# Two layers on one core: 64 tokens by fetched rows and 192 dense, with two weight parts in one stationary operand

## The reference, cut to what matters

```python
def _peer(h, w_query, sub_keys, expert_u, expert_v):
    q = (h @ w_query).reshape(B, S, PEER_HEADS, 2, PEER_KEY_DIM)      # 8 heads
    sc = jnp.einsum('bshpk,hpnk->bshpn', q, sub_keys)
    ...
    idx = jnp.take_along_axis(cand_idx, pos, axis=-1)                # 16 experts per head
    g = jax.nn.softmax(top_s, axis=-1)
    ...
        act = jax.nn.gelu(jnp.einsum('td,tkd->tk', xt, expert_u[it]))
        return jnp.einsum('tk,tkd->td', gt * act, expert_v[it])
```

## Time and profile before

| | |
|---|---|
| median of 3 runs | 1867.45 us (1861.47 to 1868.68) |
| the profiled execution | 1863.85 us |
| its span in the trace | 1862.5 us |
| mean granted TensorE clock | 0.93 |
| busy share of PE, DVE, ACT, POOL | 84%, 52%, 34%, 33% |
| DMA | 482.38 MB, 259 GB/s mean |

### The profile page before, as it was taken

The page is one execution under the profiler, slowest core; times in us unless marked ns, Lnnn a source line. Parts: engine busy times, 40 slices in busy tenths (PEclk is TensorE's granted clock), DMA queues, the critical chain, the costliest instruction groups (busy, mean ns, idle before and its releaser), DMA issues.

```text
span 1862.5 us, 21544 instructions
## 1 busy us (share of the span) xinstructions
PE 1559.8 (84%) x8662; PEld 1159.0 (62%) x8662; DVE 973.5 (52%) x1488; ACT 642.4 (34%) x924; POOL 609.5 (33%) x379
## 2 busy tenths in 40 slices
PE   6889989889888888799899999999797666666665
PEld 5677844334233323687789999999696544444443
DVE  5653512011010001566453787886227999887787
ACT  5453411001000001456453444443247634323333
POOL 3111100000000000322131434434645788888880
PEclk8988999999999999899999999999899888777777
DMA  7322578998998999444343566666862399989895
GB/s 255 115 89 68 204 288 368 422 421 357 421 421 356 422 421 407 136 142 152 113 139 133 183 209 197 205 207 198 303 194 93 136 353 345 346 314 338 304 361 222
DMA packets 110184, 482.38 MB, mean 259 GB/s; under 512 B 13808, under 2 KB 22512, under 8 KB 68480
## 3 DMA queue, kind: packets, MB, share of 16 engines
q1 hardware_dynamic: 85696, 408.04, 58.6%
q0 software_dynamic: 22528, 67.19, 10.0%
q10 hardware_dynamic: 1856, 5.72, 0.8%
HBM read 468.84 MB, written 12.06 MB: 258 GB/s over the span
## 4 chain that ended last, share of the span: by engine, by line
PE 58%; POOL 12%; DMA 10%; DVE 7%; issue 6%; ACT 6%; ACTq 0%; SPq 0%; DVEq 0%
PE ps L619 14%; PE ps L452 11%; PE ps L453 10%; PE ps L454 10%; POOL small L2307 6%; POOL big L2292 6%; DMA fix<-in_w_up 4%; PE ps L668 3%; DMA big<-in_w_up 3%; PE ps L640 2%; DMA big<-in_expert_v,tig 1%; DVE fix_parts L1040 1%; DMA fix<-in_expert_v 1%; PE ps L582 1%; PE ps L1017 1%
## 5 line engine op out<-in xcount | busy, mean ns | idle before, releaser
L454 PE MATMUL ps<-hh_parts,fix_parts 128*128 128x256 f32 x1152 | 328.6, 285 | 0.0
L619 PE MATMUL ps<-big 128*64 128x512 f32 x880 | 249.6, 602 | 30.0 <-DMA big<-in_w_up 13.2
L1040 DVE TENSOR_TENSOR fix_parts<-fix,fix_parts 128x1536 fp32r<-128x1536 f32 (+1 forms) x101 | 209.0, 2070 | 121.0 <-ACT fix_parts L1845 118.8
L1017 PE MATMUL ps<-fix_parts,y_parts 128*128 128x512 f32 x428 | 180.6, 493 | 81.6 <-DVE big_parts L1696 81.5
L1845 ACT ACTIVATE fix_parts<-fix 128x2048 fp32r<-128x2048 f32 x101 | 193.1, 1913 | 155.9 <-DMA fix<-in_expert_v 145.8
L452 PE MATMUL ps<-hh_parts,fix_parts 128*128 128x256 f32 x768 | 221.2, 288 | 20.2 <-issue 16.5
L2267 POOL TENSOR_TENSOR fix_parts<-fix,fix_parts 128x512 fp32r<-128x512 f32 x58 | 140.0, 2415 | 264.6 <-ACT fix_parts L1845 264.6
L454 PEld LDWEIGHTS ps<-hh_parts,fix_parts 128*128 128x128 f32 x1152 | 223.7, 194 | 0.0
L453 PE MATMUL ps<-hl_parts,fix_parts 128*128 128x256 f32 x768 | 219.6, 286 | 0.0
L619 PE MATMUL ps<-fix,big 128*64 128x512 f32 x656 | 197.1, 595 | 22.2 <-DMA fix<-in_w_up 7.3
L2267 POOL TENSOR_TENSOR big_parts<-big,fix_parts 128x512 fp32r<-128x512 f32 x12 | 23.7, 1974 | 546.4 <-ACT fix_parts L1845 546.4
(11 more groups left out here) (369 smaller groups left out, 3098.5 us busy)
## 6 DMA issues: line engine op xcount, KB each, us to landing
fix<-in_expert_u SPq DMA_DIRECT2D x64, 1024.0 KB, 5.1
fix<-in_expert_v SPq DMA_DIRECT2D x64, 1024.0 KB, 7.4
big<-in_w_down SPq DMA_DIRECT2D x38, 1024.0 KB, 11.1
big<-in_w_gate SPq DMA_DIRECT2D x36, 1024.0 KB, 11.1
big<-in_w_up SPq DMA_DIRECT2D x36, 1024.0 KB, 9.6
fix<-in_w_gate SPq DMA_DIRECT2D x28, 1024.0 KB, 11.2
fix<-in_w_up SPq DMA_DIRECT2D x28, 1024.0 KB, 9.6
fix<-in_w_down SPq DMA_DIRECT2D x26, 1024.0 KB, 11.1
```

The costliest lines, as they stand in the source:

```text
L454: return pe.matmul(o, l[1], r[0], start=False, stop=last)
L619: ins = pe.matmul(m.PS[64 * i:64 * i + 64, bank, :], lhs(h * k_of // 2 + k, i), view(t.place[t.slot[x]])[:, k, c0:c0 + 512], start=(h + k ...
L1017: ins = pe.matmul(m.PS[:, half, :], w[x][:, j, :], v[y][:, at:at + 512], start=(i + j + x + y == 0), stop=(i == 63 and j + x == 2), skip_g ...
L1040: nc.vector.tensor_tensor(m.fr(x[:, 0:end]), x[:, 0:end], m.fr(hi[:, 0:end]).bitcast(F32), ALU.subtract).then_inc(s.lo_v, 1)
```

## The change

The split of tokens moves from 128 and 128 to 64 and 192, and the product of the dense part is laid out anew.

- Sparse part: 64 tokens. "sparse" makes three 64x128 lists (rows, activation places, gates) in L3. ACT waits for them at tile 23 and moves them by two DMAs to a 128x64 form, so that partition t and partition 64 + t each serve half of token t's 128 experts. There are 64 fetches and 64 picks instead of 128 each. All picks are issued ahead of the fetches beyond the ring, and the ring has 5 buffers instead of 14. `sum_at` starts with step 3 and gives about one row sum to a step.
- Dense part: 192 tokens. "share" and "keys" run for block 0 too, the one-hot stage has 48 steps instead of 32, W has 192 columns an expert pair row instead of 128, and less goes to `actkeep`.
- The product over `expert_v`: ACT and DVE write the high and low parts of W (now 128x384) interleaved into WP, high, low, high, low. For the first 64 dense tokens the 128 interleaved columns are one stationary operand, and two passes (over the high and the low part of the tile) give all products. They go to two PSUM banks of their own, with a token's two parts on neighbouring partitions. The other 128 dense tokens take three passes as before, with every second column of WP as stationary operand. That is 8 + 12 = 20 matmuls a tile.
- The end: DVE copies the row sums and ACT the interleaved sums out of PSUM, and PE joins partition pairs by four matmuls with 64 columns of weights (F). Block 1's residual is added first, block 0's behind the join.

```diff
-RING = 14
+SPARSE = 64
+DENSE = 192
+RING = 5
...
-    ROUTING[_at + 22] = [("keys", _b, 0) if _b else ("sparse", 0, 0)]
+    ROUTING[_at + 22] = [("keys", _b, 0)] + [("sparse", 0, 0)] * (1 - _b)
...
-    return 1 + a * 62 // P
+    return 3 + a * 60 // SPARSE
...
-    m.W = BIG[:, 0:16384].rearrange("p (n t) -> p n t", n=128)
-    m.keys = tuple(m.tig[:, P * i:P * i + P] for i in range(3))
-    m.vix, m.aix, m.sg = m.tig[:, 384:512].bitcast(U32), m.tig[:, 512:640].bitcast(U32), m.tig[:, 640:768]
-    m.ROWS = [BIG[:, o:o + 1024] for o in [*range(24576, 32768, 1024), *range(16384, 22528, 1024)]]
-    m.ST = [BIG[:, o:o + 256].rearrange("p (n t) -> p n t", n=2) for o in (22528, 22784)]
+    m.W = BIG[:, 0:128 * DENSE].rearrange("p (n t) -> p n t", n=128)
+    m.keys = tuple(m.tig[:, DENSE * i:DENSE * i + DENSE] for i in range(3))
+    lists = m.tig[:, 3 * DENSE:768]
+    m.lists = lists.rearrange("p (x k) -> p x k", x=3)
+    m.vix, m.aix, m.sg = lists[:, 0:64].bitcast(U32), lists[:, 64:128].bitcast(U32), lists[:, 128:192]
+    m.ROWS = [DS[:, 3072 + 1024 * i:4096 + 1024 * i] for i in range(RING)]
...
+    m.ST = [yf[:, 1792 + 128 * i:1920 + 128 * i].rearrange("p (n t) -> p n t", n=2) for i in range(2)]
...
-    m.WH = [yf[:, 512 * i:512 * i + 256] for i in range(3)]
+    m.WP = [DS[:, 768 * i:768 * i + 768] for i in range(3)]
+    m.F = [EB[1][:, 1024 + 64 * i:1088 + 64 * i] for i in range(2)]
+    m.PARTS = m.ROWS[0:2]
...
-    return m.W[:, 2 * i:2 * i + 2, :].rearrange("p n t -> p (n t)")
+    two = m.fr(m.WP[i % 3]).rearrange("p (c x) -> p x c", x=2)
+    return m.W[:, 2 * i:2 * i + 2, :].rearrange("p n t -> p (n t)"), two[:, 0, :], two[:, 1, :]
...
         for what, b, _ in ROUTING.get(i, ()):
-            if what == "share" and b:
-                pe.wait_ge(s.r_share, 2)
+            if what == "share":
+                pe.wait_ge(s.r_share, b + 1)
+                if b:
+                    pe.wait_ge(s.r_keys, 1)
                 for n, src in enumerate((m.r_i1, m.r_i2, m.r_gg)):
                     ins = pe.transpose(m.PS[:, 6, n * P:(n + 1) * P], src, m.ident)
                 ins.then_inc(s.r_turned, 1)
...
-    for q in range(32):
+    for q in range(DENSE // 4):
...
-        w = [m.fr(x).rearrange("p (n t) -> p n t", n=2) for x in (m.WH[i % 3], w_tile(m, i))]
+        both = m.fr(m.WP[i % 3]).rearrange("p (j c) -> p j c", j=2)
+        w = m.fr(m.WP[i % 3]).rearrange("p (j c x) -> p j x c", x=2, j=2)
         for j in range(2):
             for half in range(2):
-                at = 1024 * j + 512 * half
+                for y in range(2):
+                    ins = pe.matmul(m.PS[:, 2 + half, :], both[:, j, 0:128], v[y][:, 1024 * j + 512 * half:1024 * j + 512 * half + 512],
+                                    start=(i + j + y == 0), stop=(i == 63 and j + y == 2), skip_group_check=True)
+        if i == 63:
+            ins.then_inc(s.half, 1)
+        for j in range(2):
+            for half in range(2):
                 for x, y in ((0, 0), (0, 1), (1, 0)):
-                    ins = pe.matmul(m.PS[:, half, :], w[x][:, j, :], v[y][:, at:at + 512],
+                    ins = pe.matmul(m.PS[:, half, :], w[:, j, x, 64:DENSE], v[y][:, 1024 * j + 512 * half:1024 * j + 512 * half + 512],
                                     start=(i + j + x + y == 0), stop=(i == 63 and j + x == 2), skip_group_check=True)
         ins.then_inc(s.used, 2)
+
+    pe.wait_ge(s.fold, 1)
+    pe.wait_ge(s.parts, 2)
+    for half in range(2):
+        for j in range(2):
+            ins = pe.matmul(m.PS[64 * j:64 * j + 64, 4 + half, :], m.F[j], m.PARTS[j][:, 512 * half:512 * half + 512],
+                            start=True, stop=True, skip_group_check=True)
+    ins.then_inc(s.joint, 1)
...
-    ve.wait_ge(s.r_keys, 1)
+    ve.wait_ge(s.r_keys, 2)
...
-    weigh(31)
+    weigh(DENSE // 4 - 1)
+    ve.wait_ge(s.ghot, DENSE // 4)
+    v.step(ve.tensor_tensor(m.F[0], m.ident[:, 0:64], m.ident[:, 64:128], ALU.add))
+    pairs = m.ident.rearrange("p (c x) -> p x c", x=2)
+    ve.tensor_tensor(m.F[1], pairs[:, 0, :], pairs[:, 1, :], ALU.add).then_inc(s.fold, 1)
 
     def w_low(i):
-        w = w_tile(m, i)
+        w, hi, lo = w_tile(m, i)
         ve.wait_ge(s.w_hi, i + 1)
-        ve.tensor_tensor(m.fr(w), w, m.fr(m.WH[i % 3]).bitcast(F32), ALU.subtract).then_inc(s.w_lo, 1)
+        ve.tensor_tensor(lo, w, hi.bitcast(F32), ALU.subtract).then_inc(s.w_lo, 1)
...
-    ve.wait_ge(s.summed, P)
+    ve.wait_ge(s.summed, SPARSE)
+    ve.tensor_copy(m.PARTS[0], SUM).then_inc(s.parts, 1)
+    ve.wait_ge(s.used, t.used[-1])
     ve.wait_ge(s.fin_in, 32)
-    for b in range(2):
-        if b:
-            ve.wait_ge(s.used, t.used[-1])
+    for b in (1, 0):
+        if b == 0:
+            ve.wait_ge(s.joint, 1)
         for half in range(2):
             xb = m.XB[:, b, 512 * half:512 * half + 512]
-            ve.tensor_tensor(xb, xb, m.PS[:, 6 - 6 * b + half, :], ALU.add).then_inc(s.y_sq, 1)
+            ve.tensor_tensor(xb, xb, m.PS[:, 4 - 4 * b + half, :], ALU.add).then_inc(s.y_sq, 1)
...
+        if b and n == 0:
+            ve.wait_ge(s.moved, 32)
...
-        ve.wait_ge(s.r_turned, 1)
+        ve.wait_ge(s.r_turned, b + 1)
+        n, to = ((SPARSE, 0), (0, P - SPARSE))[b]
         for i, dst in enumerate(m.keys):
-            ins = ve.tensor_copy(dst, m.PS[:, 6, i * P:(i + 1) * P])
+            ins = ve.tensor_copy(dst[:, to:to + P - n], m.PS[:, 6, i * P + n:(i + 1) * P])
         ins.then_inc(s.r_keys, 1)
...
     elif what == "sparse":
-        lines, quad, sums, place, diag = m.LI
-        lines = lines.bitcast(U32)
-        v.step(ve.tensor_copy(lines, m.r_i2))
-        v.step(ve.tensor_tensor(diag, m.ident, m.iota, ALU.mult))
+        h = lambda x: x[0:SPARSE]
+        i1, i2 = h(m.r_i1), h(m.r_i2)
+        lines, row, at = (h(m.L3[:, x, :]) for x in range(3))
+        u, quad, sums, place = (h(x) for x in m.LI)
...
-        v.step(ve.tensor_copy(m.sg, m.r_gg))
-        ve.tensor_copy(m.vix, sums).then_inc(s.lists, 1)
+        v.step(ve.tensor_copy(lines.bitcast(U32), sums))
+        ve.tensor_copy(at, h(m.r_gg)).then_inc(s.lists, 1)
...
+            elif what == "sparse":
+                ac.wait_ge(s.lists, 1)
+                for x in range(2):
+                    ac.dma_start(m.lists[64 * x:64 * x + 64], m.L3[0:64, :, 64 * x:64 * x + 64]).then_inc(s.moved, 16)
...
-        ac.activation(m.ST[i % 2], src[:, :, 0:P], ACT.Gelu_apprx_tanh)
-        ac.activation(m.W[:, 2 * i:2 * i + 2, :], src[:, :, P:256], ACT.Gelu_apprx_tanh).then_inc(s.act, 1)
+        ac.activation(m.ST[i % 2], src[:, :, 0:SPARSE], ACT.Gelu_apprx_tanh)
+        ac.activation(m.W[:, 2 * i:2 * i + 2, :], src[:, :, SPARSE:256], ACT.Gelu_apprx_tanh).then_inc(s.act, 1)
...
-    ac.wait_ge(s.ghot, 32)
+    ac.wait_ge(s.ghot, DENSE // 4)
...
-        ac.activation(m.fr(m.WH[i % 3]), w_tile(m, i), ACT.Copy).then_inc(s.w_hi, 1)
-
-    ac.wait_ge(s.weighed, 32)
-    ac.wait_ge(s.e_a, 32)
+        w, hi, _ = w_tile(m, i)
+        ac.activation(hi, w, ACT.Copy).then_inc(s.w_hi, 1)
...
-    ac.wait_ge(s.used, t.used[-1])
-    for b in range(2):
-        ac.wait_ge(s.y_sq, 2 * b + 2)
+    ac.wait_ge(s.half, 1)
+    ac.wait_ge(s.summed, SPARSE)
+    ac.activation(m.PARTS[1], m.PS[:, 2:4, :].rearrange("p a n -> p (a n)"), ACT.Copy).then_inc(s.parts, 1)
+    for b in (1, 0):
+        ac.wait_ge(s.y_sq, 4 - 2 * b)
...
-    po.wait_ge(s.lists, 1)
-    po.wait_ge(s.r_keys, 1)
+    po.wait_ge(s.r_keys, 2)
+    po.wait_ge(s.moved, 32)
     for k in range(RING):
         fetch(k)
     for n in range(first + 53, first + 64):
...
-    def pick(k):
-
+    for k in range(SPARSE):
         po.indirect_dma_start(m.pk[:, k:k + 1], None, acts,
                               bass.IndirectOffsetOnAxis(m.aix[:, k:k + 1], 0)).then_inc(s.picked[k // 16], 16)
-
-    for k in range(32):
-        pick(k)
-    for k in range(P):
-        if k + 32 < P:
-            pick(k + 32)
-        if k + RING < P:
-            po.wait_ge(s.summed, k + 1)
-            fetch(k + RING)
+    for k in range(RING, SPARSE):
+        po.wait_ge(s.summed, k - RING + 1)
+        fetch(k)
...
-            sy.dma_start(actkeep[:, 256 * n:256 * n + 256], m.ST[n % 2].rearrange("p n t -> p (n t)")).then_inc(s.acts_kept[n % 2], 16)
+            sy.dma_start(actkeep[:, 128 * n:128 * n + 128], m.ST[n % 2].rearrange("p n t -> p (n t)")).then_inc(s.acts_kept[n % 2], 16)
```

42 lines of the change are left out of this document (24 added, 18 removed).

## The result

| | before | changed |
|---|---|---|
| median, same chip | 1863.18 us (8 runs, 1858.82 to 1868.68) | 1872.94 us (7 runs, 1868.34 to 1883.11) |
| ratio | | 1.006, 95% interval 1.0034 to 1.0087 |
| profiled execution, its span | 1863.85, 1862.5 us | 1879.67, 1878.3 us |

An eighth run of the changed kernel fell into a slower state of the chip (1948.9 us, granted clock 0.946 for 0.964 to 0.972) and is left out of the median and the ratio. The change makes the kernel slower by 0.6%. The forecast was 1850 us, with 1832 to 1868 as its own range, so its direction is wrong and the time lies outside that range (inside the wider one of 8 in 10, 1808 to 1895). I cut the stages in all kernels at the same places: the first and the last gelu of `expert_u` on ACT, the first and the last matmul of the `expert_v` stage on PE.

The account below looks back on a forecast made before the run. It took POOL's pairs of indirect DMAs to bound the expert_v stage, with a slot ring nearly as long behind. Terms -38 + 27.4 - 14.5 + 4.8 + 0.4 + 2.3 = -17.6 gave 1850 us, range 1832 to 1868.

Parts of the forecast that it names:

- One-hots: One-hot stage: 16 more steps at 1.71 us, all on the path, +27.4 us.
- Sparse part: Last stage: POOL's 211 us saved leave the path; fetch 5 still fits, 0 to 3 us, taken as 0.
- Ring fetches: expert_u stage: five fetches hold POOL 6.6 us, PE loses 1.9 us instead of 16.4, -14.5 us.
- Lists: expert_u stage, tile 23: ACT's wait for DVE's lists delays gelus and high part, +4.8 us, from 0 to 7.
- The interleaved operand: expert_v stage: loading every second column for 12 of 20 matmuls hides under the matmuls, 0 us.
- The rival on it: expert_v stage: interleaving adds 0.8 us on PE and 0.55 on DVE a step, 1880 us in all; chance 0.09.
- PE's 20 matmuls: expert_v stage: 20 matmuls for 12 a tile, at full clock 0.23 us each, 4.6 us.
- PE at the clock of now: expert_v stage: 0.33 us a matmul, 6.6 us a tile, PE the limit, 1927 us in all; chance 0.05.
- The ring: expert_v stage: a tile's stations sum to 16.3 us, 5.4 a step over three slots, -38 us (-73 to +11).
- The ring doesn't shorten: expert_v stage: landing stays 7.4 us and DVE's queue 1.8, step 6.2, 1899 us in all; chance 0.16.
- PE full: expert_v stage: landing 5.1 us, no DVE queue, step 4.6 to 4.9 us, say 1815 us in all; chance 0.18.
- Tail: End of the kernel: four joining matmuls stand behind PE's last tile, +2.3 us, from 1 to 4.

Follow-up runs that it names:

- e14: The changed kernel with one plain float32 matmul of 512 columns on PE behind each tile's release but the last; 1868.94 us, ratio 1.0042.
- e9: The changed kernel, three slots, with 24 instead of 20 matmuls a tile; 1877.66 us against 1864.9.
- e2: The changed kernel without the 59 fetches behind the first five, row sums reusing the first rows; 1825.89 us against 1864.43.
- e1: The changed kernel with a fourth slot for expert_v tiles; 1808.11 us against 1864.43, ratio 0.9698.
- e7: The kernel before with 16 picks and 14 fetches in place of 128 each; 1809.72 us against 1860.76.
- e6: The kernel before with a fourth slot for expert_v tiles; 1857.98 us, ratio 0.9978.
- e8: The changed kernel with ACT's wait for the lists moved from tile 23 to tile 30; 1866.39 us against 1860.76.
- e11: The changed kernel with two plain float32 matmuls of 512 columns behind each tile's release but the last; 1909.98 us against 1869.17.

## Why a three-slot ring stood at 5.8 us

I took each tile's stations from the starts in the timelines of PE, ACT and DVE, for 61 tiles:

| mean, us | predicted | changed | e14 | e9 (24) | e2 (no fetch) |
|---|---|---|---|---|---|
| slot released to ACT's start (landing) | 6.4 | 6.48 | 6.29 | 5.74 | 5.15 |
| ACT high part | 1.9 | 1.91 | 1.91 | 1.91 | 1.91 |
| queue ahead of DVE | 0.5 | 0.25 | 0.17 | 0.12 | 0.07 |
| DVE low part | 2.3 | 2.29 | 2.29 | 2.29 | 2.29 |
| W's low part, hand-over | 0.6 | 0.62 | 0.62 | 0.62 | 0.62 |
| queue ahead of PE | 0 | 0.92 | 0.89 | 0.97 | 0.15 |
| PE | 4.6 | 4.95 | 4.95 | 5.60 | 4.69 |
| a third of the sum | 5.4 | 5.81 | 5.71 | 5.75 | 4.96 |

(e14's PE row has the end of the filler in it; the prediction's 6.4 is its 6.2 of landing and 0.2 of hand-overs.) The mean landing was foretold well. What the sum left out is the queue at PE, 0.92 us, in a stage where PE also idles 0.93 us a step. (That the measured stations add up to three steps proves nothing by itself: they do so in any ring, with the waiting counted in. What tells is where the waiting stands, and what a fourth slot does to it.) Both at once can only be when tiles arrive unevenly. They do, and this stretch shows how. PE first (one tile ends, a gap, the next):

```profile
1609.34 0.40 PE L1035 MATMUL ps<-x_parts,big_parts 128*128 128x512 f32 x1
1613.32 3.75 PE L1028 MATMUL ps<-fix_parts,big_parts 128*128 128x512 f32 x8 [3.59 <-DVE big_parts L1726]
1616.87 4.08 PE L1035 MATMUL ps<-fix_parts,big_parts 128*128 128x512 f32 x12
1620.79 1.53 PE L1028 MATMUL ps<-fix_parts,big_parts 128*128 128x512 f32 x6
```

ACT, which takes up a tile as it lands:

```profile
1600.00 1.92 ACT L1882 ACTIVATE x_parts<-fix 128x2048 fp32r<-128x2048 f32 x1 [6.72 <-DMA fix<-in_expert_v]
...
1608.47 1.92 ACT L1882 ACTIVATE fix_parts<-fix 128x2048 fp32r<-128x2048 f32 x1 [6.10 <-DMA fix<-in_expert_v]
...
1611.10 1.91 ACT L1882 ACTIVATE fix_parts<-fix 128x2048 fp32r<-128x2048 f32 x1 [0.28 <-DMA fix<-in_expert_v]
...
1616.70 1.91 ACT L1882 ACTIVATE x_parts<-fix 128x2048 fp32r<-128x2048 f32 x1 [3.25 <-DMA fix<-in_expert_v]
```

and DVE's row sums and POOL's fetches:

```profile
1596.17 2.68 DVE L1742 SCALAR_TENSOR_TENSOR ps<-big,small,ps 128x1024 f32<-128x1024 f32 x2
```

```profile
1597.73 0.94 POOL L2336 DMA_INDIRECT big<-in_expert_v,tig  x1 [1.33 <-DVE ps L1742]
1599.12 0.94 POOL L2336 DMA_INDIRECT big<-in_expert_v,tig  x1 [0.45 <-DVE ps L1742]
```

DVE does two row sums in a row, so POOL issues two fetches, 1.4 us apart, and the slot is released while the second is being issued, at 1599.54 (where PE is through with the tile three back). The tile lands after 8.9 us, at 1608.5, the next one 2.6 us behind it. PE has idled for 3.6 us and takes the late tile at 7.47 us for 4.6; the tile behind it has been ready for 3.6 us when PE gets to it at 1620.79. A late tile lengthens the turn of its slot, and the tile that then waits lengthens the turn of the next; an early one gives nothing back, since its slot can't be filled before PE is through.

How often? For each tile I counted the fetches whose issue on POOL ended between 2 us before its slot was released and 2.5 us before ACT's start:

| fetches beside the landing | changed | e9 (24) | e14 | e1 (four slots) |
|---|---|---|---|---|
| none | 24 tiles, 5.52 us | 18, 5.41 | 22, 5.34 | 8, 5.78 |
| one | 22, 6.64 | 34, 5.63 | 26, 6.35 | 21, 7.39 |
| two or three | 15, 7.78 | 9, 6.83 | 13, 7.77 | 31, 8.32 |
| over 6.5 us | 32 of 61 | 12 of 61 | 24 of 61 | 51 of 60 |

In the changed kernel each fetch of 0.5 MB beside a tile of 1 MB goes with about 1.1 us more of landing, and two fifths of the tiles have none beside them. These are counts within a run; the run that takes the fetches away is e2. There the landing is 5.15 us, 6.75 at most, and of queue and gaps 0.15 and 0.34 us a step are left. With four slots the landings are longer than ever, 7.7 us on average, and PE's gaps are down to 0.05 us a step: a slot more is what a ring needs to carry uneven landings.

Why 24 matmuls cost no more than 20 with three slots follows in part. In e9 PE runs without a gap from the fortieth tile on, at 5.53 us a step and landings of 5.1 to 5.7 us, though the fetches go on: PE sets the pace, the row sums keep a fixed place in it, and a fetch goes out at a moment where it meets little of a landing (34 tiles with one fetch, 5.63 us). At 20 the ring has no pace of its own, and the fetches fall anywhere. That the steady pace keeps the fetches out of the way is read from the counts, not shown by a run that moves the fetches alone; it stays open. So does why e14, with the same load on PE as e9, keeps 24 late landings for 12.

## The prediction, step by step

- *What bounds the kernel now.* Right in its first half, and shown: POOL's chain, with DVE next (e7). Its second half, a slot ring "nearly as long", doesn't hold: the 17.9 us were counted with the waiting in, which fills any ring up to three steps. With POOL's traffic gone the same three slots go round in 5.15 us a step (e7), and a fourth slot was worth 7 us (e6).
- *One-hots, +27.4.* Measured +27.8. The steps have the spacing of the earlier trace rows; in the changed kernel two neighbours start at 1485.97 and 1487.68, 1.71 us.
- *Sparse part, 0.* Right. Fetch 5 went out at 1524.48, 30 us into the last stage (26 worked out), its row sum ran at 1535.09, and DVE's row sums have 0.5 us of idle time ahead of them in the whole stage.
- *Ring fetches, -14.5.* The mechanism is right, the size was off. Against the earlier trace rows, five fetches, and the low part behind them:

```profile
1334.97 1.09 POOL L2336 DMA_INDIRECT big<-in_expert_v,tig  x1 [0.16 <-issue]
1336.37 0.94 POOL L2336 DMA_INDIRECT big<-in_expert_v,tig  x1 [0.31 <-issue]
1337.61 0.94 POOL L2336 DMA_INDIRECT big<-in_expert_v,tig  x1 [0.30 <-issue]
1338.86 1.36 POOL L2336 DMA_INDIRECT big<-in_expert_v,tig  x1 [0.30 <-issue]
1340.52 0.94 POOL L2336 DMA_INDIRECT big<-in_expert_v,tig  x1 [0.30 <-issue]
1341.48 1.28 POOL L2311 TENSOR_TENSOR fix_parts<-fix,fix_parts 128x512 fp32r<-128x512 f32 x1
```

They take 6.5 us, as 5/14 of 18.5 had it. The gelus on either side start at 1340.92 and 1350.39, 9.47 us for a pace of 5.76: 3.7 us lost, not 1.9. PE stood for 2.0 us, as worked out, and then ran at the lower clock, which the prediction had priced in brackets ("-10 if the clock falls in the short stall too") and left out of the sum. The gap and what follows it, by columns as above:

```profile
1340.95:1342.85 1.90, 0.00 (x0) 0.02 (x1) 0.00 (x0) 1.90 (x3) 1.79 (x2) 1.00 1.03 420
1342.87:1346.20 3.33, 3.33 (x15) 3.33 (x16) 1.76 (x1) 0.51 (x1) 2.75 (x1) 0.50 1.03 427
```

That is 1.8 us more than worked out, so the term is -12.7.
- *Lists, +4.8.* Measured 3.7, at the place that was named (e8). ACT's gelus came 3.7 us late, as worked out, and PE stood for 3.0 us (3.3 worked out). The other 1.5 us were for a clock that falls, and here it didn't:

```profile
1173.90:1177.00 3.10, 0.10 (x1) 0.00 (x0) 2.84 (x7) 2.58 (x4) 2.90 (x2) 1.00 0.62 172
1177.04:1182.76 5.72, 5.72 (x48) 5.72 (x49) 5.41 (x22) 0.00 (x0) 1.15 (x1) 1.00 0.26 103
```

So the lower clock was left out where it came and put in where it didn't, and that the stage's sum is right to 0.6 us is in part luck. The loss could be had back by moving the wait: 374.3 to 369.4 us. With the term above and 0.4 for the transposes the stage is -8.6 by the parts, and -8.7 as measured.
- *The interleaved operand, 0.* Right. Weight loads and matmuls over every second column (line 1035) beside those over neighbours (line 1028), min/median/max ns, against the earlier trace rows:

```profile
L1035 PEld LDWEIGHTS ps<-x_parts,big_parts x168: 193/193/334, 1505.4 to 1860.6; 128*128 128x128 f32 x168
```

```profile
L1028 PEld LDWEIGHTS ps<-x_parts,big_parts x84: 186/188/334, 1503.6 to 1857.5; 128*128 128x128 f32 x84
```

193 ns for 188, under a matmul spacing of 0.23 us: a step of two is no step of eight (330 ns). The Trainium skill (SBUF — State Buffer, Specifications, the row on cachelines) expects full rate for a step of two in float32, and this trace agrees. The rival on it falls. DVE's low part of W takes 553 ns for 384 columns, as worked out, so the interleaved writes cost nothing either.
- *PE's 20 matmuls.* 4.62 us a tile where it runs without a gap, as predicted, 4.95 on average. The rival "PE at the clock of now" falls (clock 0.94, and 1.00 in e14, where the stage is no more than 5 us shorter). The gap was there, but the earlier trace rows had shown only that one of 0.6 us does no harm; behind nine gaps of 2.7 to 4.4 us, tiles took 6.1 to 7.5 us here.
- *The ring, -38.* This step failed: the stage gave 10.7 us for 38. Landing, the parts' own times and DVE's queue came out within 0.3 us of the sum; it had no term for a queue at PE (0.92 us), and took the full clock (0.35 us). With 17.4 us for 16.3 a step is 0.37 us longer, 24 of the 27 us that were missed. I had summed means, as if tiles came evenly, while the trace of the kernel before showed uneven ones: over its last stage the time from a slot's release to ACT's start runs from 5.0 to 9.7 us, and I took the one figure of 7.4. "One fetch is nearly always beside it" was the wrong picture too: 24 of 61 tiles had none and 15 had two or three.
- *The rivals.* "The ring doesn't shorten" had the place right, and its point of decision: the change pays below 5.7 us a step, and the step is 5.82. Its causes (landing stays at 7.4, DVE's queue at 1.8) didn't happen; 6.48 and 0.25 were measured. "PE full" is what a fourth slot gives (300.9 us), by another way than the one named: the landing is 7.7 us, not 5.1.
- *Tail, +2.3.* Measured +1.9. The joining matmuls are eight records, as in the earlier trace rows:

```profile
1866.77 1.94 PE L1043 MATMUL ps<-big,hl 128*64 128x512 f32 x8
```

## What to carry to other kernels

Sum a ring of slots with its spread, not with its means: where landings vary by some microseconds (here 4.9 to 9.4, by how many indirect fetches ran beside them), a ring without a spare slot both idles and queues at its last engine, and a cut in any station's load gives back less than its share. Before work is taken off the engine that bounds a stage, ask what the ring behind it can carry, and try one slot more in the changed kernel: here the same slot was worth 7 us before the change and 71 behind it. A wait put into an engine's queue is free only where what is waited for is surely done; moving it seven tiles on was worth 5 us.

## What the runs showed of the hardware

- In the changed kernel a 1 MB load with one indirect fetch of 0.5 MB (128 rows of 4 KB) beside it landed about 1.1 us later, with two or three 2.3 us later, than the 5.5 us of a load with none; in e9, where PE sets the pace, one made 0.2 us. Without fetches (e2) loads take 5.15 us. Issued on POOL a fetch held the engine for 0.94 us in 43 of 64 cases, and for 2.7 to 2.8 us in 18.
- A float32 matmul of 512 columns on plain operands costs PE 0.87 us at the full clock, in two records, where the rounded form costs 0.23 us (e11; in e14 one of them takes the step's work from 4.62 to 5.48).
- PE's clock falls in or behind some gaps and comes back in the course of the next tile. In the last stage of the changed kernel it did so behind all nine gaps of 2.7 to 4.4 us and behind none of the shorter ones (2.3 at most); in the `expert_u` stage it fell behind a gap of 2.0 us and stayed at 1.00 behind one of 3.0 (both shown above), so the length of a gap alone doesn't tell. The stretch of the last stage shown above, by its parts (gap, eight matmuls, twelve matmuls):

```profile
1609.60:1613.30 3.70, 0.14 (x1) 0.01 (x1) 2.88 (x3) 3.42 (x4) 0.00 (x0) 0.89 0.89 313
1613.32:1616.87 3.55, 3.55 (x8) 2.78 (x9) 3.55 (x3) 0.30 (x2) 2.23 (x1) 0.50 0.18 72
1616.87:1620.79 3.92, 3.92 (x14) 3.14 (x13) 3.51 (x3) 2.20 (x2) 1.45 (x2) 0.69 0.59 147
```

The granted clock is 0.89 over the gap as a whole, 0.50 for the eight matmuls behind it (the lower of the two levels, 1.2 for 2.4 GHz), and 0.69 over the twelve, which begin at the lower and end at the higher. They took 3.55 and 3.92 us, where 20 take 4.62 at the full clock. The Trainium skill (TensorE: Matmul & The Clock Gate, Part 1) tells of the same two levels, with the lower one for an engine that has been idle; this trace agrees.
